# Scatters of a spectral convolution to partitions 4 apart, its first stage on array quarters, and a moved filter step

## The reference

```python
def hyena_filters(L, fw1, fb1, fw2, fb2, fw3, freq):
    ...
    h = (hdn @ fw3).reshape(L, HY_ORDER, 2, D_MODEL)
    decay = jnp.exp(-t * jnp.abs(deltas))
    return h * decay[:, None, None, :]

def bidir_long_conv(z, h_fwd, h_bwd, bias):
    L = z.shape[1]
    k = jnp.concatenate([h_fwd, jnp.zeros_like(h_fwd[:1]), h_bwd[1:][::-1]], axis=0)
    kf = jnp.fft.rfft(k.astype(jnp.float32), n=2 * L, axis=0)
    zf = jnp.fft.rfft(z.astype(jnp.float32), n=2 * L, axis=1)
    y = jnp.fft.irfft(zf * kf, n=2 * L, axis=1)[:, :L]
    return (y + z.astype(jnp.float32) * bias).astype(z.dtype)
...
    z = v
    for n, gate in enumerate((x1, x2)):
        z = gate * bidir_long_conv(z, filt[:, n, 0], filt[:, n, 1], fbias[n])
```

## Time and profile before

| | us |
|---|---|
| median of 3 executions | 3582.74 (3571.73 to 3589.32) |
| profiled execution | 3569.07 |
| its span | 3567.4 |
| first to last product step, M0 of round 0 to M0 of round 4 | 452.78 to 884.42 |
| M1 of round 4 begins | 930.37 |

### The profile page before, as it was taken

The page is one execution under the profiler, slowest core; times in us unless marked ns, Lnnn a source line. Parts: engine busy times, 40 slices in busy tenths (PEclk is TensorE's granted clock), DMA queues, the critical chain, the costliest instruction groups (busy, mean ns, idle before and its releaser), DMA issues.

```text
span 3567.4 us, 47950 instructions
## 1 busy us (share of the span) xinstructions
PE 3304.8 (93%) x18338; PEld 2581.6 (72%) x18338; DVE 2143.4 (60%) x3189; ACT 1313.7 (37%) x2216; POOL 313.9 (9%) x510
## 2 busy tenths in 40 slices
PE   7999889999798999999899889999999979999897
PEld 4888545555576888887788757777778758887685
DVE  6998734444466554554767555555556576655676
ACT  3212333343344333333345433333334353333344
POOL 0111234344200000000000200000000000000000
PEclk8999999999898999999999999999999989999899
DMA  7666777897701332224435310000002133333532
GB/s 294 202 200 200 214 137 155 159 170 161 253 29 57 121 95 83 80 83 176 158 97 161 128 49 15 8 7 7 7 25 77 48 110 103 104 107 118 213 98 89
DMA packets 183689, 410.15 MB, mean 115 GB/s; under 512 B 33263, under 2 KB 60207, under 8 KB 180791
## 3 DMA queue, kind: packets, MB, share of 16 engines
q1 hardware_dynamic: 131288, 270.69, 23.1%
q0 software_dynamic: 51936, 131.27, 15.5%
q10 hardware_dynamic: 288, 5.77, 0.4%
HBM read 262.51 MB, written 81.00 MB: 96 GB/s over the span
## 4 chain that ended last, share of the span: by engine, by line
PE 74%; DVE 12%; DMA 7%; ACT 3%; issue 2%; POOL 1%; SPq 1%; DVEq 0%; ACTq 0%
PE ps L624 20%; PE ps L625 19%; PE ps L626 19%; PE ps L2426 3%; PE ps L2360 2%; PE ps L2378 2%; DMA t2z<-s 2%; PE ps L2398 2%; PE ps L694 1%; DVE mx L2798 1%; DMA t2k<-s 1%; PE ps L2269 1%; DMA traw<-hidden_scratch 1%; PE ps L2461 1%; POOL t2z L1962 1%
## 5 line engine op out<-in xcount | busy, mean ns | idle before, releaser
L624 PE MATMUL ps<-HB,gsp 128*128 128x512 f32 x1232 | 489.0, 397 | 37.4 <-DVE HB L800 22.0
L625 PE MATMUL ps<-HB,gsp 128*128 128x512 f32 x1232 | 485.2, 394 | 0.0
L626 PE MATMUL ps<-HB,gsp 128*128 128x512 f32 x1232 | 483.5, 392 | 0.0
L1078 DVE TENSOR_TENSOR gsp<-graw,gsp 128x512 fp32r<-128x512 f32 x330 | 226.4, 690 | 262.4 <-ACT gsp L1057 261.7
L1057 ACT ACTIVATE gsp<-graw 128x512 fp32r<-128x512 f32 x330 | 206.6, 628 | 325.0 <-PE ps L626 266.0
L624 PEld LDWEIGHTS ps<-HB,gsp 128*128 128x128 f32 x1232 | 234.3, 190 | 90.7 <-issue 21.5
L624 PE MATMUL ps<-tsp,wdh 128*128 128x512 f32 x616 | 243.6, 395 | 38.0 <-DVE tsp L1335 37.9
L626 PEld LDWEIGHTS ps<-HB,gsp 128*128 128x128 f32 x1232 | 234.3, 190 | 49.9
L625 PEld LDWEIGHTS ps<-HB,gsp 128*128 128x128 f32 x1232 | 234.8, 191 | 46.3 <-issue 1.0
L626 PE MATMUL ps<-tsp,wdh 128*128 128x512 f32 x616 | 241.9, 393 | 0.0
L625 PE MATMUL ps<-tsp,wdh 128*128 128x512 f32 x616 | 241.8, 393 | 0.0
(11 more groups left out here) (280 smaller groups left out, 7556.6 us busy)
## 6 DMA issues: line engine op xcount, KB each, us to landing
graw<-in_w_gu SPq DMA_DIRECT2D x176, 256.0 KB, 2.7
mring<-in_mod_w POOLq DMA_DIRECT2D x78, 512.0 KB, 4.7
hidden_scratch<-R SPq DMA_DIRECT2D x154, 256.0 KB, 2.4
traw<-hidden_scratch SPq DMA_DIRECT2D x154, 256.0 KB, 2.7
t2k<-s POOLq DMA_DIRECT2D x80, 256.0 KB, 5.9
t2z<-s POOLq DMA_DIRECT2D x160, 128.0 KB, 7.9
t2w<-w POOLq DMA_DIRECT2D x160, 128.0 KB, 5.4
wd<-in_w_dx SPq DMA_DIRECT2D x6, 2816.0 KB, 15.6
```

The source lines that it names most:

```text
L624: pe.matmul(o, wh, xh, start=start, stop=False, skip_group_check=onto)
L625: pe.matmul(o, wh, xl, start=False, stop=False, skip_group_check=onto)
L626: return pe.matmul(o, wl, xh, start=False, stop=stop, skip_group_check=onto)
L1078: dve.tensor_tensor(gsp[U % 3][:, 1, :], graw[:, q, W_SLOT[i], :], gsp[U % 3][:, 0, :].bitcast(F32), ALU.subtract).then_inc(w.lo, 1)
```

## The change

Four things are done, all in the convolution.

1. **Landing partitions.** The data of one phase used to land on partitions 16 apart (`by_partition`, `t[first:P:nb]`). Now a DMA of the token rounds goes to eight partitions 4 apart, and successive DMAs alternate between the lower and the upper 64 partitions (`landing_row`, `group_row`). The constants are permuted to match. Count and size of the DMAs stay: 8 partitions, 16 rows each, 1 KB or 2 KB.
2. **First products of the filter on quarters.** `h2` had 64 zero columns and 64 zero rows; it now holds only the halves, and two units are made by four 64x64 products (line 2292 before; the `for c ... for r` loop after) into banks 0 and 1 at once. PE waits ahead of each such pair until everything in banks 0 and 1 has been taken (`pe.wait_ge(s_ae, au)`).
3. **First stages on quarters.** `filter_forward` makes a bank pair from all four units of a K step with eight 64x64x512 products, twice a step, and waits for all four units. `signal_forward` makes one bank pair for a Z unit with eight 64x64x256 products, where two full products of 512 columns ran. The results come in pairs of banks (4 and 5, then 2 and 3), which S, M's second stage and M's inverse use too, so there are new waits between those. ACT copies 1024 columns at once into four `s1` buffers instead of 512 into eight. `ksb` has six buffers instead of two, `w1` seven instead of eight.
4. **Order.** K3 moves from ahead of M1 to behind it.

```diff
+def landing_row(NB, h, c, quarter):
+    return 64 * h + (32 * c + quarter if NB == 16 else c)
+def group_row(NB, g):
+    return 64 * (g % 2) + 32 * (g // 2 % 2) + g // 4 if NB == 16 else g
...
-        STEPS += [("K", it + 1, 2), ("K", it + 1, 3)] if more else []
+        STEPS += [("K", it + 1, 2)] if more else []
         STEPS += [("M", it, 1)]
-        STEPS += [("Z", it + 1, 0), ("S", it + 1, 0)] if more else []
+        STEPS += [("K", it + 1, 3), ("Z", it + 1, 0), ("S", it + 1, 0)] if more else []
...
-        BANK_A, BANK_B = (0, 1), (2, 3)
-        SETS_C, SETS_D, SETS_S = ((4, 2), (4, 0)), ((6, 0), (6, 2)), (4, 6)
+        BANK_A, SETS_B = (0, 1), (4, 2)
+        SETS_C, SETS_D, SETS_S = ((4, 2), (6, 0)), ((6, 0), (4, 2)), (4, 6)
...
-            return t[first:P:nb, :].rearrange("p (a b) -> p a b", a=nb)[:, :, at:at + width]
+            first, step = landing_row(nb, h, c, quarter), 4 if it < NCH else 2
+            return t[first:first + step * (P // nb - 1) + 1:step, :].rearrange("p (a b) -> p a b", a=nb)[:, :, at:at + width]
...
-                if b >= 8:
-                    act.wait_ge(s_s1o[b % 8], s1_sent(b, b % 8))
-                act.activation(s1[b % 8][:], bank(BANK_B[b % 2]), ACT.Copy).then_inc(s_be, 1)
+                if b >= 4:
+                    act.wait_ge(s_s1o[b % 4], s1_sent(b, b % 4))
+                to, of = s1[b % 4][:].rearrange("p (r c) -> p r c", r=2), pair(SETS_B[b % 2])
+                if S1_SENT[b][0] == "Z":
+                    to, of = s1[b % 4][:].rearrange("p (v r c) -> p r v c", r=2, c=P), of.rearrange("p r (v c) -> p r v c", c=P)
+                act.activation(to, of, ACT.Copy).then_inc(s_be, 1)
...
+            def filter_forward(au, b, kp, which, i):
+                pe.wait_ge(s_ae, au + 4)
+                bank_b_free(b)
+                for way in range(2):
+                    for r, v in QUARTERS:
+                        mm = pe.matmul(ps[rows64(v), SETS_B[b % 2] + r, :], f1[rows64(r), which, way, rows64(r ^ i)],
+                                       ksb[2 * ((kp + v) % 3) + way][rows64(r), :], start=way == 0, stop=way == 1)
+                mm.then_inc(s_bf, 1)
+            def signal_forward(au, b, zu, which):
                 pe.wait_ge(s_ae, au + 1)
+                bank_b_free(b)
                 for h in range(2):
-                    b = b0 + h
-                    bank_b_free(b)
-                    pe.matmul(bank(BANK_B[b % 2]), f1[:, which, h, :], zsb[zu % 2][:], start=True, stop=True
-                              ).then_inc(s_bf, 1)
+                    for r, v in QUARTERS:
+                        mm = pe.matmul(ps[rows64(v), SETS_B[b % 2] + r, CW * h:CW * (h + 1)], f1[rows64(r), which, 0, rows64(h)],
+                                       zsb[zu % 2][rows64(r), CW * v:CW * (v + 1)], start=True, stop=True)
+                mm.then_inc(s_bf, 1)
...
+                        if au:
+                            pe.wait_ge(s_ae, au)
                         bank_a_free(au)
-                        pe.matmul(bank(BANK_A[au % 2]), h2[:, g0 + n2, :], fw3[kb % 2][:].rearrange("p o c -> p (o c)"),
-                                  start=True, stop=True).then_inc(s_af, 1)
+                        for c, n2 in enumerate((first, second)):
+                            for r in range(2):
+                                mm = pe.matmul(ps[rows64(c), BANK_A[r], :], h2[rows64(r), g0 + n2, :],
+                                               fw3[kb % 2][rows64(r)].rearrange("p o c -> p (o c)"), start=True, stop=True)
...
+                        forward_held(1)
+                    held += [("K", n["A"], n["B"] + i, 8 * it + 2 * o, which, i) for i in range(2)]
```

More of the change, by code:

```diff
@@ L112, in dft_constants @@
                 st[:, g, 0, col], st[:, g, 1, col] = vre, vim
+    landed, gathered = np.zeros(P, int), np.zeros(P, int)
+    slots = 64 // NB
+    for slot in range(2 * slots):
+        for i in range(NB):
+            c, rest = divmod(i, NB // 2)
+            quarter, v = divmod(rest, 2)
+            h, s = divmod(slot, slots)
+            landed[landing_row(NB, h, c, quarter) + (4 if NB == 16 else 2) * (slots * v + s)] = slot * NB + i
+            gathered[group_row(NB, i) + 4 * slot] = slot * NB + i
+    st, f1i = st[landed], f1i[gathered]
     half = [slice(32 * r, 32 * r + 32) for r in range(2)]
@@ L137, in filter_constants @@
     nt = -t[m, 0].T
-    return np.ascontiguousarray(ft), np.ascontiguousarray(nt)
+    pairs = np.zeros((P, NB), np.float32)
+    for j in range(NB // 2):
+        for v in range(2):
+            for c in range(2):
+                pairs[64 * c:64 * c + 64, 2 * j + v] = nt[64 * v:64 * v + 64, j + c * NB // 2]
+    return np.ascontiguousarray(ft), pairs
 def constants():
@@ L160, in constants @@
     as32 = lambda a: np.ascontiguousarray(a, dtype=np.float32)
-    f1 = np.zeros((P, 2, 3, P))
+    f1 = np.zeros((P, 2, 2, P))
     for i, f in enumerate((fx, fc)):
-        f1[0::2, i, 0], f1[1::2, i, 1], f1[:, i, 2] = f[0][:64], f[0][:64], f[0]
+        for v in range(2):
+            f1[:64, i, v] = f1[64:, i, v] = f[0][64 * v:64 * v + 64]
     return {
@@ L1728, in signal_part, with landing, by_group, ksb_at @@
             return (e, 0) if it < NCH else (e // 4, e % 4)
-        def by_partition(t, it, first, at, width):
+        def landing(t, it, h, c, quarter, at, width):
             nb = NBS[series(it)]
-            return t[first:P:nb, :].rearrange("p (a b) -> p a b", a=nb)[:, :, at:at + width]
+            first, step = landing_row(nb, h, c, quarter), 4 if it < NCH else 2
+            return t[first:first + step * (P // nb - 1) + 1:step, :].rearrange("p (a b) -> p a b", a=nb)[:, :, at:at + width]
+        def by_group(t, it, g, at, width):
+            nb = NBS[series(it)]
+            first = group_row(nb, g)
+            return t[first:first + 4 * (P // nb - 1) + 1:4, :].rearrange("p (a b) -> p a b", a=nb)[:, :, at:at + width]
+        def ksb_at(ku):
+            return ksb[2 * (ku // 2 % 3) + ku % 2]
         def share(t, it):
@@ L2074, in _ @@
                             act.wait_ge(s_ae, KA_AT[ku - 2] + 1)
-                        act.activation(dec[ku % 2][:], dlt[kb % 2][:, 0:CW], ACT.Exp,
-                                       scale=nt[:, g0 + n2:g0 + n2 + 1]).then_inc(s_dec, 1)
+                        act.activation(dec[ku % 2][:], dlt[kb % 2][:, 0:CW], ACT.Exp, scale=nt[:, at:at + 1]).then_inc(s_dec, 1)
+                        if u % 2 == 1 and taken < n["B"]:
+                            sent_out(taken)
+                            taken += 1
+                elif kind == "Z":
+                    for u in range(4):
                         for b in range(taken, n["B"] + u):
@@ L2079, in _ @@
                         taken = n["B"] + u
-                elif kind == "Z":
-                    for u in range(4):
-                        for b in range(taken, n["B"] + 2 * u):
-                            sent_out(b)
-                        taken = n["B"] + 2 * u
                 else:
@@ L2263, in bank_a_free, with forward_held @@
                     pe.wait_ge(s_de, EMPTIED_BEFORE["A", au])
-            def filter_forward(au, b, ku, which):
+            def filter_forward(au, b, kp, which, i):
[7 more added lines that the diff above has]
+            def signal_forward(au, b, zu, which):
                 pe.wait_ge(s_ae, au + 1)
                 bank_b_free(b)
-                pe.matmul(bank(BANK_B[b % 2]), f1[:, which, 2, :], ksb[ku % 2][:], start=True, stop=True
-                          ).then_inc(s_bf, 1)
-            def signal_forward(au, b0, zu, which):
-                pe.wait_ge(s_ae, au + 1)
                 for h in range(2):
-                    b = b0 + h
-                    bank_b_free(b)
-                    pe.matmul(bank(BANK_B[b % 2]), f1[:, which, h, :], zsb[zu % 2][:], start=True, stop=True
-                              ).then_inc(s_bf, 1)
-            held = None
+                    for r, v in QUARTERS:
+                        mm = pe.matmul(ps[rows64(v), SETS_B[b % 2] + r, CW * h:CW * (h + 1)], f1[rows64(r), which, 0, rows64(h)],
+                                       zsb[zu % 2][rows64(r), CW * v:CW * (v + 1)], start=True, stop=True)
+                mm.then_inc(s_bf, 1)
+            def forward_held(count):
+                for what, *args in held[:count]:
+                    (filter_forward if what == "K" else signal_forward)(*args)
+                del held[:count]
+            held = []
             for kind, it, o, n in WALK:
@@ L2400, in _ @@
                         mm.then_inc(s_af, 1)
[L2401 to L2403 removed]
+                        forward_held(2)
             pe.wait_ge(s_const, 1)
@@ L2669, in _ @@
                     for u in range(4):
-                        n2, cc, kb = filter_unit(it, o, u)
+                        first, second, cc, kb = filter_pair(it, o, u // 2)
                         ku, au = 16 * it + 4 * o + u, n["A"] + u
```

176 lines of the change are left out of this document (89 added, 87 removed).

## The result

The changed kernel takes 3659.70 us at the median (3656.61 to 3663.39, 4 runs), beside 3577.38 for the kernel before on the same chip. The ratio is 1.0214, 95% interval 1.0191 to 1.0237. I had forecast 3588 with a range up to 3618: slower was right only as a rival, and even that rival (3617) was 43 us too small. The profiled spans are 3655.0 and 3567.4 us, 87.6 apart.

The account below looks back on a forecast made before the run. PE, 92% busy, was taken as first limit, with the chain through POOL's scatters behind it. Terms: +4.3 us a round, +17 for four, -12 (or -8) ahead, -1 behind; forecast 3588 us, range 3552 to 3618.

Parts of the forecast that it names:

- I count +2.7 for this: In M1: +2.7 us a round for PE's lower clock in the first rows behind the idle wait ahead of M1.
- K0, B0, K1: First steps of a round: second pairs wait for emptied banks, 16.6 plus 5.2 makes 21.8 us, 0.5 less than before.
- Z1 to M1: Z1, K2, wait for M1: 6.0, copy, POOL's 9.4, landing 4.0 (bounds 2.0, 7.9) make 20.7 us instead of 24.74.
- M1: Product step M1: K2's four first stages add 2.2 and the lower clock 2.7, so 20.8 us instead of 15.90.
- K3, Z0, S0: Behind M1: S0 waits for K3's scatters until 15.8 (landing 4.0, bounds 1.7, 5.1), S0 lasts 6.1: 21.9 us, +7.6.
- A round: Sum of the parts: +8.0 us on the 104.2 us round, so 112.2; +4.3 against the average of 107.9.
- Ahead of round 0: Start up to M0 of round 0: K0 to K3 in 22 instead of 28.5, Z0 20.7 instead of 26.28; -12 us.
- Behind round 3: After the four rounds: B0's DMA wait of 0.65 goes and Z1 starts POOL a bit earlier, -1 us.
- PE's work: Convolution: PE busy some 55 us less over four rounds, while the stage hardly shortens.
- The scatters: Spread landing partitions may win back lost speed, 10.5 GB/s per engine; a queue share still near 70% would refute it.
- K3's cover is missed in full: Rival, wait ahead of M1: landings at medians, lower clock at S0; rounds of 118.7, 3617 us; 0.26 with last rival.
- above 119 a round: Sign of being wrong: rounds over 119 us mean buffers or bank waits held to be covered are not.

Follow-up runs that it names:

- e6: Changed kernel with K3 back ahead of M1, plus two groups of unused constant products between each filter step's pairs from round 1 on: 3579.9 us, 0.9993 of before.
- e1: Changed kernel plus unused constant products, two groups between filter pairs from round 1 on and ten ahead of every M1: 3632.3 us, 1.0142 of before.
- e9: As e5, with too strict waits ahead of M0 and behind filter steps relaxed: 3565.8 us, 0.9947 of before.
- e7: Kernel before with only the order of steps changed, K3 moved behind M1: 3631.0 us, 1.0145 of before.
- e8: Changed kernel with landing partitions of scatters into t2z and t2k 8 apart instead of 4: 3680.6 us, 1.0286 of before.
- e3: Changed kernel with half of Z's scatters issued by SyncE's queue instead of POOL's: 3657.1 us, 1.0201 of before.
- e5: Changed kernel with K3 back ahead of M1 and second pairs of filter steps in banks 6 and 7: 3584.6 us, 1.0011 of before.

## Why the prediction was wrong, step by step

**The step that failed** is "I count +2.7 for this": I priced the lower clock once a round, behind the long wait ahead of M1, and took the waits between the pairs of a filter step at their own length. I had read the clock behind waits of 7.77 and 9.51 us only the earlier trace rows. The trace of before holds the answer for shorter ones too, in the first 3.6 us of four product steps, behind PE waits of 2.17, 2.24, 1.75 and 1.42 us:

```profile
522.77:526.30 3.53, 3.53 (x18) 1.35 (x18) 1.23 (x1) 0.00 (x0) 0.00 (x0) 0.52 1.02 191
564.20:567.80 3.60, 3.60 (x36) 2.18 (x40) 1.29 (x2) 0.00 (x0) 0.00 (x0) 0.57 0.58 226
631.28:634.90 3.62, 3.62 (x46) 1.99 (x50) 1.60 (x2) 0.60 (x1) 0.55 (x1) 1.00 1.04 197
736.14:739.70 3.56, 3.56 (x46) 1.97 (x50) 1.54 (x2) 0.60 (x1) 0.58 (x2) 1.00 1.06 199
```

The granted clock (the number ahead of the DMA share) is 0.52 and 0.57 behind the first two, 1.00 behind the last two. I put the pair waits at 1.6 to some 3 us, four a round, so they had to be expected to bring the lower clock at least in part. With the first two rows in the sum each would have cost some 1.6 us more (3.6 us at 0.52 to 0.57 instead of 1.00; an estimate). In round 2 it was 3.4 us in K0 and B0 and 2.7 in K3, and nothing behind K1. e6 shows 3.7 a round for the pair waits alone, e1 6 with part of the long wait's clock included.

Two more terms failed beside it. The landings were too short: I took 4.0 us from POOL's end, and round 2 had 6.5 ahead of M1 and 5.8 ahead of S0, together 4.3 us. And I took the average round down to the shortest one: I had 3.7 us between the average of 107.9 and the round of 104.2, let them vanish without a row that said so, and they stayed (127.6 against 123.6 in round 2). So of the 15.4 us that a round was over, 4.0 lie there and 11.4 in round 2: some 6.1 the clock behind the pair waits, 4.3 the landings, the rest small.

- *K0, B0, K1*: forecast 21.8, measured 25.1 in round 2. The chain was right: from the first pair to the second 3.8 against my 3.75. What is over is the clock, 3.65 for the first inverse unit and 4.95 for the first stages, where I had 1.8 and 3.4.
- *Z1 to M1*: forecast 20.7, measured 24.3. POOL's rate was right; the landing behind POOL's end took 6.5 us instead of 4.0, and ACT's waits for slots of 1.2 and 2.5 us, which I had held to be covered, spread POOL's issues. The 4.0 came from round 4, the context part with other strides. My upper bound of 7.9, from the median of the earlier trace rows, was the nearer one.
- *M1*: forecast 20.8, measured 19.8. Right, with the doubled first rows.
- *K3, Z0, S0*: forecast 21.9, measured 27.7. S0 starts 20.7 behind M1, not 15.8: K3's first stages 6.13 instead of 3.4 (clock), then 5.8 from POOL's end to S0, above my upper bound of 5.1. S0 took 7.0 instead of 6.1.
- *A round*: forecast 112.2, measured 127.6. *Ahead of round 0*: forecast -12, measured -1.5; a filter step takes 6.9 us there (the second pairs of K1 to K3 begin at 407.79, 414.70 and 421.63), where I had 5.4 for its two pairs, and PE waits 5.3 ahead of S0. e9, without these pair waits, began M0 at 447.73. *Behind round 3*: forecast -1, measured +4.9; POOL ends at 1002.63 and M1 begins at 1012.45, so this landing took 9.8 where the kernel before needed 4.0. The change list ahead of the prediction speaks of the token rounds only, but the context round lands elsewhere too: on 32 partitions 2 apart in one half, where they were 4 apart over all 128. Its scatters took 9.7 us at the median instead of 5.4. Every run with the new landing has 49.2 to 52.7 from M0 to M1 in this round, the kernel before 45.95 and e7, which keeps the old landing, 46.2.
- *PE's work*: forecast some 55 us less, right in kind (at least 35 by e9), and hidden in the page of the changed kernel by the clock.
- *The scatters*: "the new partitions bring something" was right (302 to 217 us of 16 engines).
- *The rivals*: "K3's cover is missed in full" named the right place and too small a price, because it too put the clock only behind M1 and S0 and let the 3.7 us vanish. Its point of decision, 114 us a round, was passed. The last line of the prediction, above 119 a round, did come true; but slots account for a small part of it, and the clock behind the pair waits for more.

What stays open: whether the context round's new partitions are what lengthens its landing, since no run changes them alone; why the sets of the kernel before, over both halves, take some 30 us more than e8's; and what a faster issue than POOL's would bring, which e3 didn't test.

## What to carry to other kernels

A step that looks movable because its engine is the bound may be the only cover of another engine's chain: measure the chain with the step taken away (the last round, without filter steps, showed 7.77 us here) before moving it. When an edit puts many short waits on PE, price each with the clock behind it, and try first whether a second set of banks takes the wait away, which here brought a loss of 2.1% down to 1.0% and, with K3 back in its old place, made a gain of 0.5%. Where a wait is near zero ask how near the releaser is: in e9 a slower landing had no slack to use up and cost 27 us.

## What the hardware showed that I had not expected

The granted clock was 0.50 in the 3.56 us behind idle times of 2.78 and 0.89 us on PE, and 0.59 in the 6.06 us behind 2.09 and 0.89; in the kernel before it was 0.52 and 0.57 behind 2.17 and 2.24, and 1.00 behind 1.75 and 1.42. In e5 it was 0.53 behind a wait of 1.09, and the same waits of 0.83, 1.39 and 0.89 were followed by 0.57 in one round and by 1.00 in the next. Products whose result nobody reads, put between the pairs and ahead of M1, brought it from 0.85 to 0.96 over the rounds and saved 27 us. In one stretch SyncE took 1.43 us to issue a scatter that POOL issues in 0.588. With eight landing partitions side by side instead of 4 apart, for two thirds of the scattered bytes, the queue's time was 1.7 times as long.
